# Mixture-of-experts gate and up products: halves of 1408 columns in blocks of 512, 512 and 384, with 96 stationary columns

## The reference

```
def swiglu(h, w_g, w_u, w_d):
    return (jax.nn.silu(h @ w_g) * (h @ w_u)) @ w_d

def moe_swiglu(h, w_r, b_r, w_g, w_u, w_d):
    t = h.reshape(B * S, D)                       # 256 x 1024
    ...
    top_v, top_i = lax.top_k(logits, TOP_K)       # 2 of 8
    ...
    for e in range(N_EXPERTS):
        out = out + gates[:, e:e + 1] * swiglu(t, w_g[e], w_u[e], w_d[e])
```

## Time and profile before

| | us |
|---|---|
| median of 3 runs (lowest, highest) | 1311.74 (1310.15, 1314.27) |
| the profiled execution's own time | 1314.49 |
| its span | 1312.5 |
| the eight passes, from 559.6 to about 1309 | 749.9 |
| PE busy, share of the span | 1297.3, 99% |
| DVE busy | 1010.5, 77% |
| ACT busy | 830.2, 63% |

### The profile page before, as it was taken

The page is one execution under the profiler, slowest core; times in us unless marked ns, Lnnn a source line. Parts: engine busy times, 40 slices in busy tenths (PEclk is TensorE's granted clock), DMA queues, the critical chain, the costliest instruction groups (busy, mean ns, idle before and its releaser), DMA issues.

```text
span 1312.5 us, 17692 instructions
## 1 busy us (share of the span) xinstructions
PE 1297.3 (99%) x6542; PEld 1086.0 (83%) x6542; DVE 1010.5 (77%) x804; ACT 830.2 (63%) x748; POOL 144.1 (11%) x153
## 2 busy tenths in 40 slices
PE   8999999999999999999999999999999999999998
PEld 7988878888889888788878888888888888888786
DVE  7567765444466677688888888888889889888988
ACT  5555564444455555576777767777678677777774
POOL 4201010000012010110020110210200200200103
PEclk9999999999999999999999999999999999999999
DMA  9623426555576335299999999999999999999996
GB/s 341 208 98 128 161 97 194 193 191 192 193 250 199 103 128 185 85 344 363 354 398 367 373 387 377 365 379 388 370 367 381 395 368 364 411 361 370 397 360 244
DMA packets 113914, 374.98 MB, mean 286 GB/s; under 512 B 10642, under 2 KB 31294, under 8 KB 113868
## 3 DMA queue, kind: packets, MB, share of 16 engines
q1 hardware_dynamic: 106348, 365.09, 74.7%
q0 software_dynamic: 3008, 7.00, 1.5%
q10 hardware_dynamic: 4512, 2.26, 0.6%
HBM read 368.96 MB, written 7.13 MB: 287 GB/s over the span
## 4 chain that ended last, share of the span: by engine, by line
PE 78%; DVE 10%; DMA 6%; ACT 3%; issue 3%; POOL 0%; SPq 0%; DVEq 0%; ACTq 0%
PE bank L1789 33%; PE bank L1785 21%; PE bank L1786 21%; DVE wl L1251 4%; DVE wl L1237 2%; DMA ring<-in_we_gate 2%; DMA ring<-in_we_up 2%; ACT wh L870 1%; PE bank L2461 1%; DMA ring<-in_we_down 1%; DMA ring<-in_w_in 1%; ACT wh_third L870 1%; DVE scratch L1401 1%; DVE scratch L1379 1%; DVE aT_low L1256 1%
## 5 line engine op out<-in xcount | busy, mean ns | idle before, releaser
L1251 DVE TENSOR_TENSOR wl<-ring,wh 128x3072 fp32r<-128x3072 f32 (+1 forms) x127 | 402.2, 3186 | 50.7 <-PE bank L1789 27.0
L870 ACT ACTIVATE wh<-ring 128x3072 fp32r<-128x3072 f32 (+1 forms) x127 | 335.8, 2644 | 128.2 <-DMA ring<-in_we_up 40.7
L1237 DVE TENSOR_TENSOR wl<-ring,wh 128x2048 fp32r<-128x2048 f32 (+3 forms) x77 | 182.9, 2375 | 120.4 <-ACT wh L856 120.3
L1785 PE MATMUL bank<-wh,xh 128*128 128x512 f32 x608 | 238.6, 392 | 3.5 <-DVE wl L1251 3.5
L1789 PE MATMUL bank<-wl,xh 128*128 128x512 f32 x880 | 237.8, 389 | 0.0
L1786 PE MATMUL bank<-wh,xl 128*128 128x512 f32 x608 | 236.8, 389 | 0.0
L856 ACT ACTIVATE wh<-ring 128x2048 fp32r<-128x2048 f32 (+3 forms) x77 | 152.8, 1984 | 111.6 <-PE bank L1786 100.6
L1251 DVE TENSOR_TENSOR wl<-ring,wh_third 128x3072 fp32r<-128x3072 f32 (+1 forms) x64 | 184.9, 2889 | 20.5 <-PE bank L1789 9.6
L1789 PEld LDWEIGHTS bank<-wl,xh 128*128 128x128 f32 x880 | 165.2, 188 | 34.5
L870 ACT ACTIVATE wh_third<-ring 128x3072 fp32r<-128x3072 f32 (+1 forms) x64 | 153.7, 2401 | 28.4 <-DMA ring<-in_we_up 22.6
L1785 PEld LDWEIGHTS bank<-wh,xh 128*128 128x128 f32 x608 | 114.2, 188 | 29.8 <-issue 6.0
(11 more groups left out here) (290 smaller groups left out, 1699.6 us busy)
## 6 DMA issues: line engine op xcount, KB each, us to landing
ring<-in_we_down SPq DMA_DIRECT2D x56, 1536.0 KB, 8.8
ring<-in_we_gate SPq DMA_DIRECT2D x32, 1536.0 KB, 6.9
ring<-in_we_up SPq DMA_DIRECT2D x32, 1536.0 KB, 9.0
ring<-in_we_gate SPq DMA_DIRECT2D x64, 640.0 KB, 5.1
ring<-in_we_up SPq DMA_DIRECT2D x64, 640.0 KB, 6.7
ring<-in_w_in SPq DMA_DIRECT2D x8, 1536.0 KB, 7.1
ring<-in_w_gate SPq DMA_DIRECT2D x10, 1024.0 KB, 5.1
ring<-in_w_up SPq DMA_DIRECT2D x10, 1024.0 KB, 5.1
```

The source lines that it names most:

```text
L870: nc.scalar.activation(wh_in_pass(j, n), ring[:, slot, 0:n], ACT.Copy).then_inc(high_ready, 1)
L1237: nc.vector.tensor_tensor(wl[:, j, 0:n], ring[:, slot, 0:n], wh[:, j, 0:n].bitcast(F32), ALU.subtract).then_inc(low_ready, 1)
L1251: nc.vector.tensor_tensor(wl[:, j % 2, 0:n], ring[:, pass_slot(j), 0:n], wh_in_pass(j, n).bitcast(F32), ALU.subtract).then_inc(low_ready, 1)
L1785: nc.tensor.matmul(dst, x_high, w_high, start=first, stop=False)
```

## The change

It does four things inside a pass; down and everything ahead of the passes stay as they are.

- The 2816 columns are divided in the middle: halves A and B of 1408. All 16 gate and up slots have one form: gate (even) or up (odd), two feature tiles, 1408 columns of each. The slots' widths go from 3072 (eight) and 2560 (eight) to 2816 (sixteen).
- A half is computed in blocks of 512, 512 and 384 columns. A slot has 18 matmuls, 12 of 512 and 6 of 384 moving columns.
- The stationary slices of `xh` and `xl` are 96 columns wide (`0:PASS_CAP`) and not 128, and the results are written to 96 partitions. The two clearing instructions for `xh` and `xl` go. Down keeps its 128 stationary columns.
- Every slot is filled by one transfer; the eight right slots had two each.

Banks, the order of PE's turns, and the names in ACT's and DVE's work follow from it.

```diff
-    LEFT = 3 * BANK
-    RIGHT = DFF - LEFT
-    HT = LEFT // P
+    HALF = DFF // 2
+    HB = -(-HALF // BANK)
+    HT = FT // 2
...
-    HBLOCKS = {"A": [(0, 4), (4, 4), (8, 4)], "B": [(0, 4), (4, 4), (8, 2)]}
-    RIGHT_BLOCKS = ["gB0", "gB1", "mB", "uB0", "uB1"]
+    HBLOCKS = [(0, 4), (4, 4), (8, 3)]
     for n, b in (("gA0", 0), ("gA1", 1), ("gA2", 2), ("uA0", 3), ("uA1", 4), ("uA2", 5),
-                 ("gB0", 6), ("gB1", 7), ("mB", 0), ("uB0", 1), ("uB1", 2),
-                 ("hA0", 3), ("hA1", 4), ("hA2", 5), ("d0", 4), ("d1", 5),
+                 ("gB0", 6), ("gB1", 7), ("gB2", 0), ("uB0", 1), ("uB1", 2), ("uB2", 3),
+                 ("hA0", 4), ("hA1", 5), ("hA2", 4), ("d0", 4), ("d1", 5),
                  ("hB0", 6), ("hB1", 7), ("hB2", 0), ("ga0", 1), ("ga1", 3)):
...
-                    if j < KT:
-                        src = gu_rows[j % 2][:, bass.ds(e * KT + j // 2 * 2, 2), 0:LEFT]
-                        ...
-                    else:
-                        dst = ring[:, slot, 0:2 * RIGHT].rearrange("p (m c) -> p m c", m=2)
-                        for m in range(2):
-                            sp.dma_start(dst[:, m:m + 1, :], gu_rows[m][:, bass.ds(e * KT + j - KT, 1), LEFT:DFF]
-                                         ).then_inc(slot_filled[slot], 16)
+                    c0 = (j // KT) * HALF
+                    src = gu_rows[j % 2][:, bass.ds(e * KT + j % KT // 2 * 2, 2), c0:c0 + HALF]
+                    dst = ring[:, slot, 0:2 * HALF].rearrange("p (k c) -> p k c", k=2)
+                    sp.dma_start(dst, src).then_inc(slot_filled[slot], 16)
...
-            nc.gpsimd.memset(xh[:, :, PASS_CAP:P].bitcast(F32), 0.0)
-            nc.gpsimd.memset(xl[:, :, PASS_CAP:P].bitcast(F32), 0.0).then_inc(rest_cleared, 1)
...
-                                    ins = mm(lbank(f"{names}{i}")[:], xh[:, 2 * s + k, 0:P], w_low[:, c:c + BANK], False, False)
+                                    ins = mm(lbank(f"{names}{i}")[0:PASS_CAP, 0:n], xh[:, 2 * s + k, 0:PASS_CAP],
+                                             w_low[:, k * HALF + a:k * HALF + a + n], False, False)
...
-                left_slots(*range(KT))
-                right_slots(8, 9)
+                gate_up_slots(*range(9))
                 hidden_transposed("A", 0, 1)
-                right_slots(10)
+                gate_up_slots(9, 10)
                 hidden_transposed("A", 2)
-                right_slots(*range(11, 2 * KT))
+                gate_up_slots(*range(11, 16))
                 down_slots(16)
```

More of the change, by code:

```diff
@@ L1678, in rows_added, with up_times_gate @@
                                                              ALU.mult, ALU.add))
[L1680 to L1694, removed]
+                def up_times_gate(half, *banks):
+                    for i in banks:
+                        a, b = i * BANK, min(i * BANK + BANK, HALF)
+                        c = "AB".index(half) * HALF
+                        dve.wait_ge(*lfull(f"u{half}{i}", p))
+                        dve.wait_ge(*ltaken(f"g{half}{i}", p))
+                        nc.vector.tensor_tensor(h1[0:PASS_CAP, c + a:c + b], lbank(f"u{half}{i}")[0:PASS_CAP, 0:b - a], h1[0:PASS_CAP, c + a:c + b], ALU.mult
+                                                ).then_inc(ltake(f"u{half}{i}"), 1)
                 def hidden_low(half, *blocks):
                     for i in blocks:
-                        j0, k = HBLOCKS[half][i]
+                        j0, k = HBLOCKS[i]
                         j = "AB".index(half) * HT + j0
@@ L1719, in expert_pass @@
                 lows(7, 8)
-                left_hidden()
+                up_times_gate("A", 0, 1, 2)
                 lows(9, 10)
@@ L2370, in _, with gate_up_slots @@
             rounds = pe.value_load(npass[0:1, 0:1], min_val=1, max_val=ROUNDS)
-            pe.wait_ge(rest_cleared, 2)
+            pe.wait_ge(rest_cleared, 1)
             def expert_pass(p, e, last):
-                def right_slots(*slots):
+                def gate_up_slots(*slots):
                     for j in slots:
[L2375 to L2403, removed]
@@ L2404, in left_slots @@
+                        s, half = j % KT // 2, "AB"[j // KT]
+                        names = "gu"[j % 2] + half
+                        w_high, w_low = wh_in_pass(j, 2 * HALF), wl[:, j % 2, 0:2 * HALF]
+                        cols = [(i, i * BANK, min(BANK, HALF - i * BANK)) for i in range(HB)]
                         pe.wait_ge(high_ready, p * PASS_FILLS + (NSPLIT + j + 1))
@@ L2427, in left_slots @@
                             for k in range(2):
-                                for i in range(HB):
+                                for i, a, n in cols:
                                     if (k, i) == (1, HB - 1):
@@ L2441, in left_slots @@
                             pe.wait_ge(low_ready, p * PASS_FILLS + (NSPLIT + j + 1))
[L2442 to L2443 removed]
+                            for i, a, n in cols:
+                                ps = lbank(f"{names}{i}")[0:PASS_CAP, 0:n]
                                 for k in range(2):
[L2445 to L2446 removed]
+                                    ins = both(ps, xh[:, 2 * s + k, 0:PASS_CAP], xl[:, 2 * s + k, 0:PASS_CAP],
+                                               w_high[:, k * HALF + a:k * HALF + a + n], False)
                                 if i == HB - 1:
@@ L2480, in down_slots @@
                                 for half, j0 in (("A", 0), ("B", HT)):
-                                    for b, (first_, _) in enumerate(HBLOCKS[half]):
+                                    for b, (first_, _) in enumerate(HBLOCKS):
                                         if j == j0 + first_:
```

63 lines of the change are left out of this document (26 added, 37 removed).

## The result

| | before | after |
|---|---|---|
| median of 6 runs each, on one chip (lowest, highest) | 1314.38 (1310.15, 1315.72) | 1323.09 (1320.39, 1323.85) |
| the profiled execution's own time | 1314.49 | 1320.39 |
| eight passes, sum of their lengths | 749.89 | 754.01 |
| a pass in which PE never waits | 92.53 to 92.55 | 93.43 to 93.49 |

The changed kernel takes 1.007 times as long, 95% interval 1.0057 to 1.0083: some 9 us slower. Predicted were 1372 us, 60 us above the median shown there, with a range of its own from 1354 to 1386; the direction was right and the size was not. One execution among all those of this document, 1433.93 us at a granted clock of 0.851 in the run of 96 columns with widths grouped, was slow and is left out of its median.

The account below looks back on a forecast made before the run. PE's instruction stream was taken to set the end. 64.0 us for 96-column matmuls less 3.5 of stalls gave 60.5 on 1314.49: 1375.0, as a median 1372; own range 1354 to 1386, 8-in-10 range 1290 to 1386.

Parts of the forecast that it names:

- The bound: In the passes PE's instruction stream sets the end; the question is how often PE can start the next matmul.
- I take 40 ns: Gate/up matmuls with 96 stationary columns: 40 ns beside their columns, 8.0 us more a pass, 64.0 in all; chance 0.48.
- the plain 13.3 ns row: Trace before: fp32r matmuls with 128 stationary columns take 13.3 ns beside their columns, at 256 and 512 moving columns.
- The number of matmuls: Gate and up go from 264 to 288 matmuls; 24 more at 13.3 ns cost 0.32 us a pass, 2.6 over eight.
- the 4 ns that the earlier trace left open for the 384 form: Matmuls of 384 moving columns might take 177 ns, not 173.3; that would add 0.35 us a pass, 2.8 in all.
- Stalls given back: PE's waits for late low parts of the weights vanish because slots get 8% longer: 3.5 us taken off.
- The zeros: DVE and ACT work, turns one slot earlier, transfers and two dropped POOL clearings were each costed at zero.
- Nothing changes: Rival: 96-column matmuls in gate and up keep 13.3 ns beside their columns; +2.6 to +5.4 us, 1314 to 1317; chance 0.21.
- Hidden: Rival: the 96-column weight load runs beside the stream, leaving 2.4 ns a matmul; 22.6 us less, about 1292; chance 0.12.
- shrinks with the columns: Rival: the exposed load falls with fewer stationary columns, to 10 ns a matmul; -5.1 us, 1307; chance 0.07.
- 80 ns: Rival: a plain 96-column load is wholly exposed in each gate and up matmul; +156 us less 3.5, 1464; chance 0.04.

Follow-up runs that it names:

- the kernel of one width: New split with 128 stationary columns, every 384-column block computed as one of 512; 1353.36 us, ratio 1.0294 to the kernel before.

## Why the prediction was wrong

**The bound.** Right. PE is 99% busy before and after, clean passes have no idle PE, and what a matmul costs beside its columns is the question.

**The step that failed** is "I take 40 ns" for 96 stationary columns: the term of 8.0 us a pass, 64.0 in all. Worked out as the prediction does, an instruction with 512 moving columns now has 229.9 - 213.3 = 16.6 ns beside its columns, one with 384 has 174 - 160 = 14; put into the prediction's sum, 192 x 16.6 + 96 x 14 = 4.5 us against 3.52, that is 1.0 us a pass and not 8.0. The 40 came from the loads' modelled lengths and from reading 13.3 ns as a special fast load that only 128 columns have; 124 columns run at the same 226.7 ns. The run with 96 alone (+0.74 us a pass, where 40 ns would be 264 x 26.7 ns = 7.0) and the streams with 32 to 124 stationary columns (226.7 to 233.3 ns for 512) show that there is no such step at 128. A 96-column operand shows some 3 ns more than one of 128; how much of the 13.3 and the 16.6 is load no run here tells. Ahead of the result, the plain 13.3 ns row, the nearest in kind, deserved more than the 0.21 it got. Why the distance is 226.7 and not 213.3 stays open.

**The number of matmuls.** 24 x 13.3 ns = 0.32 us a pass is right as a count, and it is what the kernel of one width bears out (97.95 against 92.53 + 24 x 0.2267 = 97.97). But 13.3 ns was taken as fixed for any mixture of widths. It belongs to an undisturbed stream of one width. Mixed with 384s, 128 stationary columns cost 1.04 us a pass more: the split by itself costs 1.41. That term was not among the prediction's; only the 4 ns that the earlier trace rows left open for the 384 form pointed to it. Those five matmuls are the second half of ten that stand behind matmuls of another form, and their starts lie 182, 173, 173 and 174 ns apart: a first distance still unsettled, in the trace of before.

**How the two parts come to +0.9.** In the new kernel 192 matmuls of 512 columns cost 3.2 ns more than 226.7, 0.61 us; 96 of 384 some 0.6 ns more than 173.3, 0.06; the 24 added ones 0.32. Together 0.99 us; the clean passes show 0.88 to 0.96. With 96 stationary columns the mixture costs nothing further, so the narrower operand, which costs 0.74 in the old split, here takes the place of a cost of 1.04. Eight passes: +7.0 to +7.7, less the stalls given back.

**Stalls given back.** Taken off: 3.5 us. Measured: 2.3 us less idle PE in the passes. The reason given (slots 8% longer) didn't come about; slots are 1% longer. Which part of the change did it was not isolated. PE waits 3.5 us for the low part in the passes of the kernel before, 1.2 in the changed one, 0.4 to 1.8 in the seven variants whose passes are 0.5 to 1.7 us longer, and not at all in the one whose passes are 5.4 us longer. So slower slots may be the reason even at 1%; but each of these is one execution.

**The zeros** for DVE and ACT, the turns, the transfers and POOL held, the first three with their rows above; POOL's busy time fell by 4.3 us on the page, and PE waits for it no more than before.

**The rivals.** "Nothing changes", +2.6 to +5.4 us, was nearest but ends below the 9 us found. "Hidden" and "shrinks with the columns" fall: no number of stationary columns went below 226.7 ns with 512 moving ones. "Shrinks" would have held at 256 moving columns (120.0 ns with 128, 113.3 with 64), a width that this product doesn't use. "80 ns" falls further.

## What to carry to other kernels

- In a stream that PE alone bounds, look at the distances between single starts, not only at their mean. An even 226.7 ns is a rhythm that can be lost: here 96 rather than 128 stationary columns lose 3 ns a matmul, and alternating 512 and 384 columns with 128 stationary ones some 3.6 ns.
- Keep one width through a block if the number of matmuls is not raised by it. If widths must be mixed, grouping them didn't help here: 93.95 to 93.85 us a pass with 128, none with 96.
- Do not read the cost of a weight load from the modelled length of its record; a stream of 24 of the instructions in question, run by itself, gives it directly. Run it behind more than one kind of neighbour: with 100 stationary columns the answer was 226.7 or 233.3 ns by what stood before.

## What the runs showed of the hardware

- fp32r, 128 stationary columns, one width, settled distance by moving columns: 512 226.7; 496 220; 480 216.7; 464 210; 448 202.7 in one run and 206.7 in another; 432 about 196; 416 188.3; 400 180.0; 384 173.3; 352 161.1; 320 146.7; 288 131.7; 256 120.0 ns. Beside the columns at 0.4167 ns that is 13.3 at 512, 496, 400, 384, 320 and 256, but 16.7 at 480, 16 or 20 at 448 and 11.7 at 288. So 128 stationary columns have two lasting rhythms too, at 448 if not at 512.
- 512 moving columns, by stationary columns: 128 and 124 226.7; 112 229; 104 228.9; 100 226.7 or 233.3; 120 233.3; 96 and 64 230; 32 231.7 ns. 256 moving columns: 128 120.0; 120 117; 96 116; 64 and 32 113.3.
- With 100 stationary columns the kernel changed from 226.7 to 233.3 ns in the middle of a pass in six of seven passes, each time at the slot whose low part came late; the smallest lateness of a start that went with it is 8 ns. What the rhythms are made of stays open.
- The version that would beat both kernels did not show up: none of the streams with 512 moving columns settled faster than the kernel before already runs.
